# Token sum T3 moved from GpSimd to VectorE, and one plain feed-forward pair moved ahead of the blocks

## What is computed

```python
# first layer: the gates, 3 * 1024 output columns
h = rms_norm(x, pre_norm_w[l])
p = h @ w_cat
gates = jax.nn.sigmoid(p_gate.reshape(bsz, slen, N_BRANCH, D_MODEL))
merged = jnp.einsum('bsnd,nbsd->bsd', gates, proj)
# second layer: feed-forward, D_FF = 2816 = 22 * 128
m = rms_norm_2(h, ffn_norm_w[l])
h = h + (jax.nn.silu(m @ w_gate[l]) * (m @ w_up[l])) @ w_down[l]
```

## Time and profile before

| | us |
|---|---|
| median of 3 runs | 2319.93 (2318.32 to 2322.87) |
| the profiled execution's own time | 2326.09 |
| its span, first to last instruction | 2324.3 |
| TensorE busy | 2273.7 (98%) |
| VectorE busy | 1404.9 (60%) |
| ScalarE busy | 780.1 (34%) |
| GpSimd busy | 555.1 (24%) |
| granted TensorE clock, mean | 0.993 |

### The profile page before, as it was taken

The page is one execution under the profiler, slowest core; times in us unless marked ns, Lnnn a source line. Parts: engine busy times, 40 slices in busy tenths (PEclk is TensorE's granted clock), DMA queues, the critical chain, the costliest instruction groups (busy, mean ns, idle before and its releaser), DMA issues.

```text
span 2324.3 us, 31121 instructions
## 1 busy us (share of the span) xinstructions
PE 2273.7 (98%) x12512; PEld 1868.5 (80%) x12512; DVE 1404.9 (60%) x2264; ACT 780.1 (34%) x1304; POOL 555.1 (24%) x387
## 2 busy tenths in 40 slices
...
GB/s 150 46 54 50 63 54 41 63 49 57 70 109 94 117 110 224 253 135 132 71 73 49 39 50 46 33 123 113 64 82 82 82 82 82 76 216 64 84 138 71
DMA packets 245951, 208.56 MB, mean 90 GB/s; under 512 B 44080, under 2 KB 217776, under 8 KB 245808
## 3 DMA queue, kind: packets, MB, share of 16 engines
...
## 4 chain that ended last, share of the span: by engine, by line
PE 84%; DVE 11%; issue 2%; DMA 1%; ACT 1%; POOL 1%; SPq 1%; DVEq 0%; ACTq 0%
PE PS L120 81%; PE PS L123 3%; DVE Ntmp L129 1%; DVE Nn L129 1%; SPq L146 1%; POOL sm L129 0%; DVE ro L129 0%; DVE Yt L137 0%; DVE sm L1969 0%; DVE T1f L129 0%; DVE Wlo L129 0%; DMA HloF<-in_w_out_dram 0%; DMA g_row<-in_pre_norm_w_dram 0%; DVE ST L137 0%; DVE smx L2155 0%
## 5 line engine op out<-in xcount | busy, mean ns | idle before, releaser
L120 PE MATMUL PS<-Hhi,Whi 128*128 128x512 f32 (+1 forms) x1544 | 498.0, 391 | 2.9 <-DVE qb L137 1.3
L120 PE MATMUL PS<-Hhi,Wlo 128*128 128x512 f32 (+1 forms) x1544 | 496.7, 390 | 2.3 <-DVE Wlo L129 2.3
L120 PE MATMUL PS<-Hlo,Whi 128*128 128x512 f32 (+1 forms) x1544 | 498.4, 391 | 0.0
L120 PEld LDWEIGHTS PS<-Hhi,Whi 128*128 128x128 f32 x1544 | 284.7, 189 | 61.9 <-issue 4.9
L120 PEld LDWEIGHTS PS<-Hhi,Wlo 128*128 128x128 f32 x1544 | 284.8, 189 | 58.5 <-DVE Wlo L129 2.7
L120 PEld LDWEIGHTS PS<-Hlo,Whi 128*128 128x128 f32 x1544 | 284.7, 189 | 57.7 <-issue 4.9
L126 ACT ACTIVATE Whi<-Wraw 128x512 fp32r<-128x512 f32 x222 | 138.3, 623 | 552.4 <-PE PS L120 548.9
L129 DVE TENSOR_TENSOR Wlo<-Wraw,Whi 128x512 fp32r<-128x512 f32 (+1 forms) x140 | 118.5, 847 | 185.2 <-ACT Whi L126 184.6
L129 POOL TENSOR_TENSOR Wlo<-Wraw,Whi 128x512 fp32r<-128x512 f32 x82 | 123.0, 1500 | 418.9 <-ACT Whi L126 418.5
L120 PE MATMUL PS<-YMhi,Wlo 128*128 128x512 f32 (+1 forms) x328 | 108.4, 382 | 8.3 <-DVE Wlo L129 8.3
L120 PE MATMUL PS<-YMlo,Whi 128*128 128x512 f32 (+1 forms) x328 | 107.9, 381 | 0.0
...
## 6 DMA issues: line engine op xcount, KB each, us to landing
Wraw<-in_w_in_dram SPq DMA_DIRECT2D x126, 256.0 KB, 2.9
...
```

Source lines behind the costliest of these rows:

```text
L120: return self.h.matmul(out, lhsT, rhs, start=start, stop=stop, skip_group_check=True)
```

## The change

T3 goes to VectorE in both parts: in part f its three passes and the lo half, in part g the lo half. GpSimd's stream `block_tokens`, its letter in `ORDER` and the signal `comb_pool` are gone. One plain pair moves from behind the blocks to ahead of them: pairs 0, 1, 2 are plain, blocks are f = 3 to 20, and pair 21 alone stands behind. VectorE makes the sums of part f in another order. `ORDER` and `PICKS` are written anew for all engines and the whole program.

```diff
-PLAIN_G, PLAIN_F = [(1, d) for d in range(4)], (0, 1, 20, 21)
+PLAIN_G, PLAIN_F = [(1, d) for d in range(4)], (0, 1, 2, 21)
-BLOCKS_F = [("f", f) for f in range(2, 20)]
+BLOCKS_F = [("f", f) for f in range(3, 21)]
+OPEN = {"g": BLOCKS_G[0], "f": BLOCKS_F[0]}
-N_BACK["f"] = N_RG_LAST + 4 + 4 * len(PLAIN_F) // 2
+N_BACK["f"] = N_RG_LAST + 4 + 4 * OPEN["f"][1]
...
-        for tile in plain(1):
+        for tile in plain(1) + plain(2):
             yield from dense([tile], K.YMhi, K.YMlo, m_ready, dps=three)
         for b in BLOCKS_F:
             yield from block_products(b)
-        for tile in plain(20) + plain(21):
+        for tile in plain(21):
             yield from dense([tile], K.YMhi, K.YMlo, m_ready, dps=three)
...
-                pe.wait_ge(*(S.comb_pool if block == "T3" else S.comb_dve).at((kind, "lo", block)))
+                pe.wait_ge(*S.comb_dve.at((kind, "lo", block)))
...
-            for name in ("T2", "T3", "T1", "T4") if kind == "g" else ("T1", "T2", "T4", "T3"):
-                act.wait_ge(*(S.comb_pool if (kind, name) == ("f", "T3") else S.comb_dve).at((kind, name)))
-                if kind == "f" and name in ("T1", "T2"):
-                    act.wait_ge(*S.comb_dve.at((kind, {"T1": "T2", "T2": "T4"}[name])))
+            for name in ("T2", "T3", "T1", "T4") if kind == "g" else ("T2", "T1", "T3", "T4"):
+                act.wait_ge(*S.comb_dve.at((kind, name)))
...
-            for step in ("T1", "+T1", "T2", "+T2", "T4", "T3", "+T3", "lo T2", "+T4", "lo T1", "lo T4") if kind == "g" else (
-                    "T1", "+T1", "T2", "+T2", "T4", "+T4", "lo T2", "lo T1", "lo T4"):
+            for step in ("T1", "+T1", "T2", "+T2", "T4", "T3", "+T3", "lo T2", "+T4", "lo T3", "lo T1", "lo T4") if kind == "g" else (
+                    "T1", "+T1", "T2", "+T2", "T4", "lo T2", "T3", "+T3", "lo T1", "lo T3", "+T4", "lo T4"):
...
-    def block_tokens():
-        for kind in "gf":
-            B, T3 = K.bp[kind].blocks, K.bp[kind].comb["T3"][:]
-            if kind == "f":
-                pool.wait_ge(*S.nlo_dve.at(("F", 7, 1)))
...
-            pool.tt(B["T3"][1], T3, B["T3"][0].bitcast(F32), ALU.subtract).then_inc(*S.comb_pool.tick((kind, "lo", "T3")))
-            yield
...
-        sp.wait_ge(*S.ffn_dve.at(("fb", 19)))
+        sp.wait_ge(*S.ffn_dve.at(("fb", 20)))
...
-        "d2mcsdcsdcsd2csdscdsdscmdcd22gd53sd4sd3sd4s2d2scd3cs2cd4cd4cd3cd4cd3cd41gd683n2d12n2d12n2d19n2d23n2d"
+        "d5s2d4scmdcs2cdsd2csdscdsd2csmcd4cd21gd53sd3sd3sd5s2d2scd3cs2cd5cd4cd3cd4cd3cd35gd684n2d12n2d12n2d19"
```

More of the change, by code:

```diff
@@ L749, in block_products @@
                 "c": S.ffn_dve.at(("v", b)), "d": S.ffn_dve.at(("u1", b)), "e": S.ffn_dve.at(("g2", b))}
-        for name, block, out in P.first if b in (BLOCKS_G[0], BLOCKS_F[0]) else P.products:
+        for name, block, out in P.first if b in OPEN.values() else P.products:
             first = out not in bank
@@ L1631, in block_weights @@
             kind, P = b[0], K.bp[b[0]]
-            start = b[1] == (2 if kind == "f" else 0)
+            start = b == OPEN[kind]
             for c, (name, _, _) in enumerate(P.products):
@@ L2560, in block_weights @@
                 yield
-    def block_tokens():
-        for kind in "gf":
-            B, T3 = K.bp[kind].blocks, K.bp[kind].comb["T3"][:]
-            if kind == "f":
-                pool.wait_ge(*S.nlo_dve.at(("F", 7, 1)))
-                pool.wait_ge(*S.nhi_act.at(("F", 7, 1)))
-                pool.wait_ge(*S.dense_pe.at(("tile", ("F", 7))))
-                pool.tt(T3, B["B22"][0].bitcast(F32), B["B12"][0].bitcast(F32), ALU.subtract).then_inc(*S.comb_pool.tick())
-                yield
-                for x, op in (("B22", ALU.add), ("B12", ALU.subtract)):
-                    pool.wait_ge(*S.comb_pool.last())
-                    pool.tt(T3, T3, B[x][1].bitcast(F32), op).then_inc(*S.comb_pool.tick((kind, "T3")))
-                    yield
-            pool.wait_ge(*S.comb_act.at((kind, "T3")))
-            pool.tt(B["T3"][1], T3, B["T3"][0].bitcast(F32), ALU.subtract).then_inc(*S.comb_pool.tick((kind, "lo", "T3")))
-            yield
     return {"w": weights(), "q": token_norms(), "p": prep(), "g": group_norm(), "t": projections(), "m": out_weights(),
             "n": norms(), "k": key_stream(), "o": rotations(), "x": attention(0), "y": attention(1), "z": attention(2),
-            "r": retention(), "u": hidden(), "S": block_weights(), "T": block_tokens()}
+            "r": retention(), "u": hidden(), "S": block_weights()}
 def sync_program(K, sp):
@@ new lines @@
+        "a7d26a2d9ad2ad14ad14ad13ad13ad3ad2ad100pd5pd8pd20id4pd17sdsd2sdsd4id5pd4sd6pd11pd23id57pd4id5sd3sd3s"
+        "d5s2d3sdcd3scsdscd2sdcsdscdscd3cpcd19pd3gd7pd21id9pd8id5sd3sd3sd5s2d3scd3cs2cdsd2csdsdcsdscd4cpcd4pd"
+        "17pgd18id12pd4id4sd3sd3sd5s2d2scd3cs2cdsd2csdsd2csdscd3cpcd18gd33pd5sd2psd3sd5s2d2sd2cd2scsdpcd3cd3c"
+        "d3cd3cd3cd10sdsd2sdsd2gd4id5id5pd4sd5pd8pd25id60pd3m2d2sd3id4sd4sd5s2d3scd3cs2cdsd2csdscdsdscd4cpdcd"
+        "4pd10pd6gd17id26pd4id5sd3sd3smd3s2d2scmd2cs2cdsd2csdscdsdscd4cpdcd3pd11pd10gd12id30pdmdmd2sd3id4sd3s"
@@ new lines @@
+        "yt2x2d7yd4yd5w3d111n2d10n2d13n2d9ndnd21n2d24n2d24n2d37n2d1152o2d21o2d21o2d21o2d21o2d21o2d26o2d19od13"
+        "o",
+    "act":
+        "w3q3a3qawqa2qaqaqa9w2ewewep5wpwepw2es2ws2pwpfpsp2w2pfwpw3fw2fws3wsfs7ws2pgwep4wgwepwpwews3ws6ws4p2gw"
+        "fp3wgpwfpw2fs2ws7ws4pwgwfgw2ep4ws2pswes3ps2w2egs2ws2gwfp3swp2wfpwpw3fw2fwf2swfs4ws8wep5gwpgwepw2ew2f"
+        "s3fs2wsfs7wfp5wgpwfgpw3f3wfs3ws3fs4ws3f2wgwfgfw2f2w2f2sws5wfs2fw2tSgw2tgTStS2TS3tTSTtS3t3S3t2S4tS2t2"
+        "StStS3tStStStStS3tStStStStS3tStStStStS3tStStStStS3tStStStStS3tStStStStS3tStStSt2b3wbwtwt2wtw3b2w2b2w"
+        "3b2wlwbwlbw6mwm2wm2wm2wm2wm2wm2wm3n3h2n2h2n2h2nh2n2h2n2h2n2h2n2h2r3w2kwkvwv2kw2kwk2wokw2v3k2rw2ox3y2"
+        "xwyz2yzwk2x2wxrkxr3zry2cywox2kyxz2xwkzy2zwvy2x2v2xcrxw2oy2z2yzwyzwk2x2rxr2xrkwry3zwzoyzkwzwvcvz2vzk2"
+        "x2rzwx2kcwox2y2xwxyz2ywk2zrkzwr4x2woxy2kz2wyxyzwvcvy2vzyrywx3ywyk2oxz2y2zwzkcwz2kzwr2zkx2kx2y3wyckx2"
+        "y2xdxyz2yd2z2wdcwiwdi3wd2i3din2h4n2h4nh2nh2nh2nh2Sw2uwSwST2w2uw2TS2uTS3uS5u2S2uS4uSuS2uS4uSuS2uS4uSu"
+        "S2uS4uSuS2uS4uSuS2uS4uSuS2uS4uSuS2uS4uSuS2uS4uSuS2uS4uSuS2uS4uSuS2uS4uSuS2uS4uSuS2uS4uSuS2uS4uSuS2uS"
+        "4uSuSuw2uwuw2H3wuHwH2wH2wH2wuH2wH2wuHw2uw2uw2uw2uw2uw2uH3wHwH2wHw25",
```

88 lines of the change are left out of this document (36 added, 52 removed).

## The result

| | before | after |
|---|---|---|
| median, us | 2320.66 (4 runs, 2318.32 to 2322.87) | 2294.64 (4 runs, 2292.88 to 2296.51) |
| the profiled execution, its span | 2326.09, 2324.3 | 2292.88, 2291.1 |
| mean granted clock | 0.993 | 0.998 |

The ratio is 0.9888, 95% interval 0.9871 to 0.9905: 26.0 us less, where the prediction had 12.9 and its range ended at 20.9 less. The direction was right, the size was not. Two repetitions further down gave 0.9888 and 0.9890. One execution of the kernel before, in the first series of experiments, took 3223.5 us at a mean granted clock of 0.652; it is left out of every ratio.

A forecast was written before the change was run, and what follows sets the result against it. The prediction took TensorE, busy 98% of the span, as the bound, so only its waits and clock could give time. Terms 10.2 + 0.8 + 1.9 = 12.9 us, from 2319.9, gave 2307.0 us, range 2299 to 2317.

The forecast's parts named there:

- T3 off GpSimd in part f: Opening of part f: TensorE's 8.26 us wait for Wlo and 1.9 us of low clock go, together 10.2 us.
- The sign "0.7" for wS: Opening of part f: if the forecast is right, VectorE's wS takes 0.7 us, where it took 5.0.
- T3 onto VectorE: Part f: four passes, 9.2 us, behind the awaited splits; 54 us of work in 67, so nothing is late.
- xu at 0.8: Part f: TensorE's 1.6 us wait for xu stays in part; 0.8 us gained, bounds 0 and 1.6.
- The pair behind the blocks: Hidden state's refill, covered by one pair fewer: thinnest margin 1.4 us, no loss taken, bounds 0 and 5 us loss.
- T3lo in part g: Opening of part g: the 2.27 us wait goes, gx's grows 0.4; net 1.9 us gained, bounds 0 and 2.3.
- The new order of the interleaved stages: Both interleaved stages, tables rewritten: 0 gained, bounds 8 us gained (a third of 25 us idle) or 8 lost.
- idle time off by more than 8: Sign that the forecast is wrong: idle time in the two interleaved stages off 25 us by more than 8.
- The slower rival: Interleaved stages: TensorE comes too early at small matmuls, losing 21.5 us against 12.9, so 2328.5 us; chance 0.08.
- the new interleaving gives back most: Two interleaved stages: 4 to 7 more waits of 2 us, 8.2 to 17 us, 2315.3 to 2324; chance 0.12.
- Port time wherever the sum is made: Part f: T3's passes on VectorE hold up TensorE's awaited work; total gain only 7.2 us, 2312.7; chance 0.05.
- The base of 2319.9: Whole kernel: median of the runs before, in us, from which the prediction subtracted its summed gain of 12.9.

The follow-up runs named there:

- f_pair2: Kernel before with the plain pair moved ahead of part f's blocks and VectorE's sums reordered, but T3 there whole on GpSimd: 2325.20 us, ratio 1.0004.
- f_t3only: Kernel before with T3 of part f on VectorE, plain pairs left at two ahead and two behind: 2322.43 us, ratio 0.9993.
- s_first: Kernel before with all engines' changed order in the first interleaved stage and part g's opening alone, T3's lo half there on GpSimd: 2318.64 us, ratio 0.9973.
- a_gpool: Changed kernel with T3's lo half of part g back on GpSimd at its old place: 2301.93 us, ratio 0.9903 to the kernel before.
- s_both: Kernel before with the changed orders of both interleaved stages, part f as before: 2311.58 us, ratio 0.9952.
- g_shift: Kernel before with TensorE's order alone altered: group norm's transposes 6 large-matmul steps later in five of eight units: 2326.68 us, ratio 1.0015.
- f_all2: Kernel before with only part f as changed, its PSUM banks renamed to avoid a clash at the final projection: 2312.36 us, ratio 0.9948.

## Why the prediction was right and where it failed

- **T3 off GpSimd in part f**, 10.2 us: right, in mechanism and size. The stretch gave 10.27, T1f, wS and T2f came to 2.3, 1.8 and 2.3 us. f_pair2 shows that the engine, not the room, was the cure for that wait. The sign "0.7" for wS was not met, since fSlo stayed on GpSimd.
- **T3 onto VectorE**, nothing late: right, and f_t3only shows the pair was needed: 7.2 us of wait without it. xu at 0.8: the number is right (0.78), the reason less so. The prediction left it at half because of a shared bank, and took the half from the earlier trace rows, whose 0.79 is the wait for gx. f_pair2 has 0.8 and f_t3only 1.6, so the wait fell with the third pair.
- **The pair behind the blocks**, refill 0: right; the margin was 2.8 us where 1.4 were forecast.
- **T3lo in part g**, 1.9 us: 2.55 between the profiles, some 3.5 by the ratios of runs. The wait of 2.27 us went, as said. The 0.4 us more for gx did not come (0.80 after, 0.79 before), and the split came 4.9 us earlier against block 0, not "some 8", which was enough. Missing was that with the new order the same pass on GpSimd costs more, and by another wait, for GpSimd's own split (3.6 us in s_first, 5.7 in a_gpool's profile).
- **"The new order of the interleaved stages", "I take 0", bounds 8 either way: the step that failed.** It was worth 11.2 us (s_both), the greater part of the 13.1 us that the forecast was short. Three things were wrong in it. The bound was put on idle time alone, "a third of the 25 us of idle", and 10.5 of 25 went: the prediction's own sign, idle time off by more than 8, was met. The clock in these stages was put at nothing, although had shown what can come with a wait: each of the five dips took 1.7 us more, so the stages held 25 + 8.5 = 33.5 us. (A third of that would have been 11, but nothing stands behind the third; the agreement is luck.) And the argument for 0 fails in the very unit that it looked at. It has TensorE asking 2.7 us earlier for a `Yt` that is 2.29 us earlier, so the wait of 2.10 us would have grown to 2.5; it fell to 1.02:

```profile
696.69 0.66 PE L123 MATMUL PS<-cst,Yt 128*128 128x128 f32 x4 [2.10 <-DVE Yt L129]
```

```profile
685.13 0.65 PE L123 MATMUL PS<-cst,Yt 128*128 128x128 f32 x4 [1.02 <-DVE Yt L129]
```

g_shift shows besides that a group read by itself doesn't give the sign, since its wait can go to the next group. Why the new tables have less idle time stays open.
- **The slower rival** (TensorE too early at the small matmuls) and "the new interleaving gives back most" did not happen: five waits for `Yt`, 10.3 us, became three, 3.2 us. In the other direction g_shift, which put TensorE later, gained nothing either.
- **Port time wherever the sum is made**: f_all2's 12.1 us (9.3 to 15.1), against 4.5 + 0.8 for that rival in part f, settles it. The Trainium skill's warning in "Perfetto Trace Analysis", section "Optimizing Scalar/DVE Operations", that moving work between the two might not help, is not borne out for this move: back on VectorE the passes on T3 take 2.3 us each in part f, where GpSimd has no pass of 128x2048 left to run beside them.
- The base of 2319.9, three runs, is low: in 72 further runs the medians were 2322 to 2325. It shifts the time by 2 to 5 us, but hardly the ratio, and the error is in the gain.
